# A pair of attention scores and one turning of weights, each moved one weight unit later in a two-block transformer kernel

## What is computed

```python
def hybrid_mixer(u, positions, w_in, b_gate, w_branch_moba, w_branch_sb, w_out):
    proj = u @ w_in
    q_a, k_a, v_a, q_b, k_b, v_b, g_a, g_b = jnp.split(proj, cuts, axis=-1)
    q_a = partial_rotary(split_heads(q_a, N_HEADS_MOBA), positions)
    k_a = partial_rotary(split_heads(k_a, N_HEADS_MOBA), positions)
    y_a = merge_heads(moba_attention(q_a, k_a, split_heads(v_a, N_HEADS_MOBA)))
    y_b = merge_heads(stick_breaking_attention(...))
    gates = jax.nn.sigmoid(jnp.concatenate([g_a, g_b], axis=-1) + b_gate)
    merged = gate_a * (y_a @ w_branch_moba) + gate_b * (y_b @ w_branch_sb)
    return merged @ w_out
```

## Time and profile before

| | us |
|---|---|
| median of 3 runs | 1198.92 (1198.78 to 1199.03) |
| the profiled execution | 1198.96 |
| its span in the profile | 1197.1 |
| TensorE busy | 1190.7 (99%) |
| DVE busy | 782.6 (65%) |
| ACT busy | 705.6 (59%) |

### The profile page before, as it was taken

One profiled execution on the slowest core, in us unless ns is written; L12 is line 12 of the kernel. 1 busy time (PEld: TensorE's weight loads), 2 busy tenths in 40 slices (PEclk: granted clock), 3 DMA queues, 4 the chain that ended last, 5 costly groups with the idle time before them and its releaser, 6 DMA issues.

```text
span 1197.1 us, 16770 instructions
## 1 busy us (share of the span) xinstructions
PE 1190.7 (99%) x5582; PEld 983.5 (82%) x5582; DVE 782.6 (65%) x1113; ACT 705.6 (59%) x1035; POOL 74.1 (6%) x119
## 2 busy tenths in 40 slices
PE   9999999999999999999999999999999999999998
PEld 7888888777788888888888788888888888888887
DVE  6655655798676555656778756755656666765554
ACT  7655555776656554557766567655555556655552
POOL 0430000000000000001220110000000000000000
PEclk9999999999999999999999999999999999999999
DMA  9977765795476888755656528977755453876662
GB/s 323 275 225 235 223 197 157 195 186 183 142 224 186 255 252 235 223 171 168 201 172 181 176 70 236 251 225 218 211 168 176 141 181 104 263 225 200 202 198 76
DMA packets 229176, 237.34 MB, mean 198 GB/s; under 512 B 76864, under 2 KB 169152, under 8 KB 229120
## 3 DMA queue, kind: packets, MB, share of 16 engines
q1 hardware_dynamic: 163792, 214.61, 57.2%
q10 hardware_dynamic: 63536, 16.26, 8.2%
q0 software_dynamic: 1792, 5.75, 1.6%
HBM read 219.78 MB, written 1.05 MB: 184 GB/s over the span
## 4 chain that ended last, share of the span: by engine, by line
PE 95%; ACT 1%; DVE 1%; DMA 1%; issue 1%; ACTq 0%; POOL 0%; SPq 0%; POOLq 0%
PE bank L2149 29%; PE bank L2151 29%; PE bank L2150 29%; PE bank L2208 2%; DMA sb_qkT<-sb_qkT 1%; PE bank L2356 1%; PE bank L2611 1%; DVE sb_wl L1444 1%; PE bank L2628 1%; PE bank L2372 1%; PE bank L2343 1%; ACT sb_wh L761 1%; PE bank L2341 0%; ACTq L1041 0%; PE bank L2310 0%
## 5 line engine op out<-in xcount | busy, mean ns | idle before, releaser
L1444 DVE TENSOR_TENSOR sb_wl<-sb_raw,sb_wh 128x1024 fp32r<-128x1024 f32 x313 | 376.4, 1222 | 122.9 <-ACT sb_wh L761 117.7
L2149 PE MATMUL bank<-sb_wh,sb_aTh 128*128 128x512 f32 (+1 forms) x1124 | 435.8, 388 | 0.5 <-DVE sb_aTl L1866 0.4
L2151 PE MATMUL bank<-sb_wh,sb_aTl 128*128 128x512 f32 (+1 forms) x1124 | 430.9, 383 | 0.0
L2150 PE MATMUL bank<-sb_wl,sb_aTh 128*128 128x512 f32 (+1 forms) x1124 | 430.7, 383 | 0.0
L761 ACT ACTIVATE sb_wh<-sb_raw 128x1024 fp32r<-128x1024 f32 (+1 forms) x319 | 327.1, 1047 | 154.1 <-PE bank L2151 101.2
L2149 PEld LDWEIGHTS bank<-sb_wh,sb_aTh 128*128 128x128 f32 x1124 | 211.2, 188 | 42.6 <-DVE sb_aTl L1866 0.8
L2151 PEld LDWEIGHTS bank<-sb_wh,sb_aTl 128*128 128x128 f32 x1124 | 211.2, 188 | 41.8
L2150 PEld LDWEIGHTS bank<-sb_wl,sb_aTh 128*128 128x128 f32 x1124 | 211.4, 188 | 40.2
L1444 DVE TENSOR_TENSOR sb_wl<-sb_z,sb_wh 128x1024 fp32r<-128x1024 f32 x88 | 107.4, 1225 | 55.9 <-ACT sb_wh L761 55.8
L881 ACT ACTIVATE sb_junk<-bank,sb_rstd 128x256 f32<-128x256 f32 x88 | 37.0, 471 | 156.9 <-PE bank L2151 156.7
L1507 DVE SCALAR_TENSOR_TENSOR sb_scores<-bank,sb_rstd,sb_junk 128x256 f32<-128x256 f32 x88 | 38.5, 479 | 118.1 <-ACT sb_junk L881 118.1
(11 more groups left out here) (231 smaller groups left out, 930.3 us busy)
## 6 DMA issues: line engine op xcount, KB each, us to landing
sb_raw<-ffn_w_down SPq DMA_DIRECT2D x80, 256.0 KB, 4.4
sb_raw<-w_in SPq DMA_DIRECT2D x80, 256.0 KB, 3.7
sb_raw<-w_down SPq DMA_DIRECT2D x80, 256.0 KB, 3.9
sb_raw<-w_gate SPq DMA_DIRECT2D x48, 256.0 KB, 3.2
sb_raw<-w_up SPq DMA_DIRECT2D x48, 256.0 KB, 3.9
sb_raw<-ffn_w_gate SPq DMA_DIRECT2D x44, 256.0 KB, 3.6
sb_raw<-ffn_w_up SPq DMA_DIRECT2D x44, 256.0 KB, 4.4
sb_raw<-e_w_in SPq DMA_DIRECT2D x40, 256.0 KB, 3.3
```

The lines of the kernel that those rows point to most:

```text
L1444: dve.tensor_tensor(wl[:, u % NSPLIT, :], raws[SLOT[u]], wh[:, u % NSPLIT, :].bitcast(F32), ALU.subtract).then_inc(low_done, 1)
L2149: pe.matmul(dst, lh, w_hi, start=start, stop=False)
L2150: pe.matmul(dst, lh, w_lo, start=False, stop=False)
L2151: return pe.matmul(dst, ll, w_hi, start=False, stop=stop)
```

## The change

Two numbers in two lists:

```diff
-        MIX_SCORES = [13, 17, 21, 25, 29, 32, 35, 38]
-        MIX_T = [17, 18, 21, 22, 25, 26, 29, 30, 32, 33, 35, 36, 38, 39, 40, 41]
+        MIX_SCORES = [14, 17, 21, 25, 29, 32, 35, 38]
+        MIX_T = [17, 19, 21, 22, 25, 26, 29, 30, 32, 33, 35, 36, 38, 39, 40, 41]
```

## The result

| | before | after |
|---|---|---|
| median of 21 runs each, us | 1198.73 (1198.09 to 1200.11) | 1200.46 (1199.75 to 1202.48) |
| ratio to before | | 1.0015, 95% interval 1.0009 to 1.0022 |
| span of the profiled execution, us | 1197.1 | 1199.2 |

The change makes the kernel 1.7 us slower (1.1 to 2.6 by the interval). The median is inside the prediction's bound of 0.2%, which is 2.4 us; the upper end of the interval is just past it. Forecast were 1200.1 us and no change beyond that bound, with a range of 1198.1 to 1201.3.

The account below looks back on a forecast made before the run. The prediction took TensorE's work plus its waits to bound the kernel. A removed wait of -0.70 us and a new one of +1.95 gave +1.25, say +1.2, on 1198.92: 1200.1 us, range 1198.1 to 1201.3.

Parts of the forecast that it names:

- The gain of 0.70 us: TensorE before the first scores: its wait for VectorE's join L1628 goes, gaining 0.70 us (bounds 0.63 to 0.78).
- The chain on VectorE and ScalarE: Second head's weights move behind the rotation: its L1077 comes 5.13 us later, the next pair's Abs 3.12 us late.
- The issue of the transpose: ScalarE's copy of the second head's turned weights queues behind a DMA transpose issue of 2.93 us, adding 0.17 us.
- TensorE's wait: After unit 22, before L2356: TensorE waits 1.95 us for ScalarE's copy sb_probsT, 0.2 of it already at unit 21.
- unit 23's low half: VectorE's split for unit 23: ready at 255.2, wanted by TensorE at 257.2, so 2.0 us to spare.
- The first premise: Whole kernel: TensorE is busy 1190.7 of 1197.1 us, so an edit without added work only removes or makes its waits.
- Only the wait goes: Rival: unseen slack of 2 us on ScalarE or VectorE, so only the 0.70 us gain shows, 1198.2 us; chance 0.12.
- The long issue: Rival: transpose issue holds ScalarE 4.76 us, total +3.1, 1202.0 us; chance 0.09 for 4.1 or more, 0.15 for 3.3 to 4.1.
- A unit's low half: Rival: VectorE over 2.0 us later than found, unit 23's low half missing on TensorE, 1201 to 1203 us; chance 0.05.

Follow-up runs that it names:

- the look: One more profiled execution of the kernel with first-pair scores moved behind unit 14, second-head turning left behind unit 18, against the kernel before: 1202.8 us.

## Why the prediction was right, and where it was right by luck

The time was forecast as +1.25 us and came to +1.73. The place and the mechanism of the loss were right. Two terms were off, one by 0.70 us and one by 0.23, and their errors partly cancel: that the forecast is within 0.5 us is in part luck. That the time stays inside the bound is not; with both terms right it would as well.

**The gain of 0.70 us: wrong.** The step that failed is the first one: a wait read in one trace was taken for the kernel's. Its releaser was a DMA, and the term should have been about 0 with 0.70 as its end. With it the sum misses by 0.70.

**The chain on VectorE and ScalarE: right.** Counted from TensorE's first scores (forecast at 228.28, measured at 228.91), the second head's weights came after 9.58 us forecast and 9.59 measured, its L1077 after 11.80 and 11.81, ScalarE's Abs of the next pair after 15.54 and 15.46. The idle time on ScalarE was put at some 4.3 us and was 4.20.

**The issue of the transpose: mis-sized.** It was to hold ScalarE for 2.93 us and to cost 0.17; it held it for 1.83, and VectorE released the L1077 behind it (0.78 us idle). The Trainium skill's sentence (DMA: Bandwidth & Descriptors, "Issuing engines are not separate DMA queues"), by which such an issue is usually small relative to the DMA, gave the better value for this term, 0; but 1.83 us of the 5.8 to landing is not small, it was only covered. The prediction took 2.93 because the surroundings of this transpose would shift with it. They did not: in the six traces in which ScalarE gets to the issue early the same one takes 2.50 to 3.39 us, in the eight in which it gets there late 1.81 to 2.09. The core's DMA engines were busy for 0.97 of the time during the issue in the trace of before and for 0.34 in that of after. That the lighter traffic is what makes the issue short is likely, but no run here tests it.

**TensorE's wait: 1.95 forecast, 1.72 lost.** The copy came 27.76 us after the first scores instead of 28.13: 0.17 of that is the issue, 0.08 had been gained by the Abs, and 0.10 lies between the copy into sb_yTh and this one (0.36 before, 0.26 after), which the prediction shifted as it stood. Of these 0.37 us the wait kept 0.14: TensorE started 0.62 behind the start of the copy instead of 0.52, and was itself ready 0.04 earlier. The prediction had 0.2 us of the wait at unit 21 already; there was none, as the copy was done at 250.70 and TensorE's L2372 comes at 251.62. Behind it the forecast held: no second wait, and unit 23's low half in time.

The sum with the terms as measured, 0 + 1.72, is the measured +1.73.

**The first premise** was that an edit without added work can only remove a wait of TensorE or make one. It held for this change. The half with the later scores alone shows a third way: behind a wait the granted clock can fall, and the same matmuls then take 1.6 us longer.

**The rivals.** "Only the wait goes" is out: there was no slack, and in most traces there was no wait to go. The long issue didn't occur; the issue was shorter, not longer. A unit's low half was never missing in any of the traces. One rival was missing in the prediction: that the wait before the first scores is not there in most executions. One trace of before could not tell, but its row says that the join had waited for a DMA's landing, and that should have raised the question. It would have moved the forecast to +1.95, 1200.9, inside the range.

**No faster version** came out of it. With the step put back ahead of the rotation the later scores cost nothing and give nothing (0.9990 to 1.0008).

## What to carry to other kernels

When a step is moved one iteration later in hand-written engine lists, look at what it is now queued behind on each engine, not at its consumer alone: here a step of 2.1 us on VectorE came behind a rotation that itself waits for ScalarE, and ScalarE then stood idle for 4.2 us with unrelated work behind it. The two engines hand work to each other here, and VectorE was busy for 94% of this stretch, ScalarE for 74%. The delay ran on nearly undiminished: allowing for the 0.63 us by which the whole trace is later, it was 3.0 us at the Abs of the next pair and 2.9 at the copy six units on, where it reached the engine that sets the time. That place is found by adding up rows. A wait that ends with a DMA's landing should be seen in more than one execution before its removal is counted as a gain. And a time that is longer than the waits explain is a reason to look at the granted clock behind the longest wait.

## What the runs showed of the hardware

One pause of TensorE of 2.29 us is enough to bring its granted clock from 1.00 to 0.5 for the matmuls behind it, in 9 of 13 executions of the same kernel (timed ones and the look), at a cost of 1.7 to 2 us; pauses of 1.56 us (22 executions of the changed kernel) and of 1.80 us (10 executions) didn't do it once. I had not counted on the clock at all. By the Trainium skill (TensorE: Matmul & The Clock Gate, Part 1) there are these two levels, 1.2 and 2.4 GHz, and idleness brings the lower one; the rows agree, with matmuls of 512 columns 0.43 us apart at the one and 0.23 at the other. So the cost of a wait is not smooth in its length: from some length on the clock is added.

The same DMA transpose of 128 x 2048 two-byte values holds ScalarE's queue for 1.8 us and lands after 5.8 where it is issued at 247.8 us or later (seven traces), and for 2.1 to 3.4 us, landing after 5.9 to 8.5, where it is issued earlier (seven traces). I take it that it meets fewer weight loads when VectorE's splits, which free the buffers, are late; no run tried that.
